# First expert layer: gate and up weights in blocks of 128 rows by 2048 and 1536 columns, and overflow products at the head of every other chunk

## The reference, cut to what matters

```python
def swiglu(h, w_in, w_out):
    gate, up = jnp.split(h @ w_in, 2, axis=-1)
    return (jax.nn.silu(gate) * up) @ w_out

for e in range(N_EXPERTS):          # 8 experts, D_FF = 3584
    y = y + gates[:, e:e + 1] * swiglu(hf, w_in[e], w_out[e])
```

## Time and profile before

| | |
|---|---|
| median of three runs | 1984.08 us (1981.81 to 1988.30) |
| span of the profiled execution | 1985.8 us; the page gives no other time of it |
| TensorE matmuls busy | 1831.9 us, 92% |
| VectorE, ScalarE, GpSimd busy | 610.9, 479.7 and 350.8 us |
| read from HBM | 579.96 MB, 293 GB/s over the span |
| mean granted TensorE clock | 0.954 of full speed |

### The profile page before, as it was taken

How to read it: one execution, slowest core, us unless ns; L and a number is a source line. 1 busy time by engine, 2 the same in 40 slices (tenths; PEclk the granted TensorE clock), 3 DMA queues, 4 the chain that set the end, 5 groups by cost and what they waited for, 6 DMA issues and landing times.

```text
span 1985.8 us, 28964 instructions
## 1 busy us (share of the span) xinstructions
PE 1831.9 (92%) x12157; PEld 1071.5 (54%) x12157; DVE 610.9 (31%) x1257; ACT 479.7 (24%) x813; POOL 350.8 (18%) x306
## 2 busy tenths in 40 slices
PE   8999999998996999999999999999995887699996
PEld 7987999776974433334333333233322887544442
DVE  6777545347465200100000000010002685600101
ACT  5854444315422110001000010000001564322120
POOL 3000000000000699999900000000001000000000
PEclk9998999998998899999999999999998897889999
DMA  6455665436525999999999999999995440579995
GB/s 187 154 147 179 207 204 204 159 119 243 193 89 211 391 410 405 419 413 410 404 416 416 410 410 397 419 410 411 404 420 189 140 152 11 212 288 419 419 420 234
DMA packets 185008, 583.04 MB, mean 294 GB/s; under 512 B 11162, under 2 KB 77355, under 8 KB 158241
## 3 DMA queue, kind: packets, MB, share of 16 engines
q1 hardware_dynamic: 182256, 575.09, 75.3%
q0 software_dynamic: 2608, 5.97, 1.1%
HBM read 579.96 MB, written 1.05 MB: 293 GB/s over the span
## 4 chain that ended last, share of the span: by engine, by line
PE 72%; DMA 12%; DVE 10%; ACT 3%; issue 2%; SPq 0%; DVEq 0%; ACTq 0%
PE ps L1708 18%; PE ps L435 8%; PE ps L436 8%; PE ps L437 8%; DMA ring<-in_moe_w_out 7%; PE ps L2147 6%; PE ps L1713 5%; PE ps L1744 4%; DMA ring<-in_moe_w_in 3%; PE ps L2171 3%; DVE wlo L468 2%; PE ps L1749 1%; DMA more<-in_moe_w_in 1%; PE ps L604 1%; PE ps L2114 1%
## 5 line engine op out<-in xcount | busy, mean ns | idle before, releaser
L1708 PE MATMUL ps<-ring,xg 128*64 128x512 f32 x1624 | 411.3, 602 | 13.0 <-ACT sgm L1818 5.8
L468 DVE TENSOR_TENSOR wlo<-raw,whi 128x2048 fp32r<-128x2048 f32 (+6 forms) x97 | 213.8, 2208 | 190.0 <-ACT whi L460 189.8
L1708 PEld LDWEIGHTS ps<-ring,xg 128*64 128x64 f32 x1624 | 122.2, 137 | 219.3 <-issue 207.8
L460 ACT ACTIVATE whi<-raw 128x2048 fp32r<-128x2048 f32 (+6 forms) x97 | 178.8, 1845 | 182.3 <-PE ps L437 80.6
L435 PE MATMUL ps<-xh,whi 128*128 128x272 f32 (+1 forms) x712 | 212.1, 298 | 4.4 <-DVE xl L535 4.3
L1744 PE MATMUL ps<-ring,ahm 128*64 128x512 f32 x824 | 204.5, 598 | 11.4 <-DMA ring<-in_moe_w_out 8.9
L437 PE MATMUL ps<-xh,wlo 128*128 128x272 f32 (+1 forms) x712 | 209.7, 295 | 0.0
L436 PE MATMUL ps<-xl,whi 128*128 128x272 f32 (+1 forms) x712 | 209.4, 294 | 0.0
L2080 POOL TENSOR_SCALAR lnt<-lnt,h 128x384 f32<-128x384 f32 x120 | 188.3, 1569 | 12.2
L1882 DVE TENSOR_TENSOR sgm<-sgm,ps 128x512 f32<-128x512 f32 x28 | 18.2, 685 | 512.0 <-PE ps L1713 512.0
L715 POOL DMA_DIRECT2D lnt<-in_ln_gain x4 | 2.2, 559 | 819.7 <-issue 524.9
(11 more groups left out here) (572 smaller groups left out, 2439.6 us busy)
## 6 DMA issues: line engine op xcount, KB each, us to landing
ring<-in_moe_w_in SPq DMA_DIRECT2D x203, 1024.0 KB, 17.9
ring<-in_moe_w_out SPq DMA_DIRECT2D x103, 1024.0 KB, 19.9
ring<-in_w_gate SPq DMA_DIRECT2D x29, 1024.0 KB, 13.4
raw<-in_ffn_w_in SPq DMA_DIRECT2D x28, 1024.0 KB
ring<-in_w_down SPq DMA_DIRECT2D x26, 1024.0 KB, 13.0
raw<-in_w_ada SPq DMA_DIRECT2D x24, 1024.0 KB
more<-in_moe_w_in SPq DMA_DIRECT2D x21, 1024.0 KB, 18.1
ring<-in_w_up SPq DMA_DIRECT2D x20, 1024.0 KB, 11.6
```

The lines of the kernel that those rows point to most:

```text
L460: e.activation(whi[0:rows, s % NSPL, 0:n], raw[0:rows, i % NRAW, 0:n], ACT.Copy).then_inc(S.hi.s, S.hi.up((s,)))
L468: e.tensor_tensor(wlo[0:rows, s % NSPL, 0:n], raw[0:rows, i % NRAW, 0:n], whi[0:rows, s % NSPL, 0:n].bitcast(F32), ALU.subtract).then_inc( ...
L1708: e.matmul(ps_[b][64 * v:64 * v + 64, :], a[:, kk_, 64 * v:64 * v + 64], both[v][:, k, 512 * b:512 * b + 512], start=kk_ == 0, stop=kk_ == 7)
```

## The change

There are two column groups now, 2048 and 1536 wide, and a chunk of gate or up is one block of 128 rows: 8 KB or 6 KB in one piece to a partition. A pass has 16 steps of the first and 16 of the second group, and 14 of down as before. Gate and up of the first group take five PSUM banks each. The overflow products of a chunk are four matmuls of 512 or 384 columns, in place of eight of 256 or sixteen of 128. In every other step (j odd), in down too, the overflow products come first and the main ones after them. The hidden tiles `sgm` and `sgo` are twice as large, and transposes are done once after the first group and once in down.

```diff
-GROUPS = [(0, 1024), (1024, 1024), (2048, 1024), (3072, 512)]
+GROUPS = [(0, 2048), (2048, 1536)]
...
-                o, m = o + (3584 if nm == "u" else 0), 2048 // n
-                part = lambda v: w_in[bass.ds(v, 1), 128 * m * j:128 * m * j + 128 * m, o:o + n].rearrange("e (k p) n -> p (e k) n", p=128)
+                o, m = o + (3584 if nm == "u" else 0), 1
+                part = lambda v: w_in[bass.ds(v, 1), 128 * j:128 * j + 128, o:o + n].rearrange("e (k p) n -> p (e k) n", p=128)
...
-            return a[:, 256 * c:256 * c + 256] if n == 1024 else a.rearrange("p (j q i) -> p j i q", j=2, i=2)[:, c // 2, c % 2, :]
+            return a[:, 512 * c:512 * c + 512] if n == 2048 else a.rearrange("p (s j q i) -> p j i s q", j=2, q=128, i=2)[:, c // 2, c % 2]
...
+                    ps_, po = [], None
+                    for j in range(8):
+                        both = pair_weights(e, C, SLOTS1, (key, x, nm, gi, j), 1)
+                        for what in ("mo", "om")[j % 2]:
+                            if what == "o":
+                                po = po or bk.take(e, key, nm + "o", x, gi)
+                                for c in range(4):
+                                    ins = e.matmul(po[32 * c:32 * c + 32, 0:n // 4], a[:, j, 128:160], quarter(both[0][:, 0, :], n, c),
+                                                   start=j == 0, stop=j == 7)
+                                continue
                             for b in range(n // 512):
+                                if j == 0:
+                                    ps_.append(bk.take(e, key, nm, x, gi, b))
                                 for v in range(2):
+                                    ins = e.matmul(ps_[b][64 * v:64 * v + 64, :], a[:, j, 64 * v:64 * v + 64],
+                                                   both[v][:, 0, 512 * b:512 * b + 512], start=j == 0, stop=j == 7)
...
                 both = pair_weights(e, C, SLOTS1, (key, x, "d", 0, j), 2)
+                for what in ("mo", "om")[j % 2]:
...
                 if j == 0:
-                    turn(x, 3)
+                    turn(x, 1)
```

More of the change, by code:

```diff
@@ L259, in chunk @@
                 o, n = GROUPS[gi]
-                o, m = o + (3584 if nm == "u" else 0), 2048 // n
-                part = lambda v: w_in[bass.ds(v, 1), 128 * m * j:128 * m * j + 128 * m, o:o + n].rearrange("e (k p) n -> p (e k) n", p=128)
-            pieces = lambda s, v: [(s.rearrange("p (k n) -> p k n", k=m), part(v))]
-            S.add((key, x, nm, gi, j, u), 128, CW, pieces, split=False)
+                o, m = o + (3584 if nm == "u" else 0), 1
+                part = lambda v: w_in[bass.ds(v, 1), 128 * j:128 * j + 128, o:o + n].rearrange("e (k p) n -> p (e k) n", p=128)
+            w = CW if nm == "d" else n
+            pieces = lambda s, v: [(s[:, 0:w].rearrange("p (k n) -> p k n", k=m), part(v))]
+            S.add((key, x, nm, gi, j, u), 128, w, pieces, split=False)
         for x in range(NP1):
-            steps = [(nm, gi, j) for gi, (_, n) in enumerate(GROUPS) for nm in "gu" for j in range(n // 256)]
+            steps = [(nm, gi, j) for gi in range(len(GROUPS)) for nm in "gu" for j in range(8)]
             steps += [("d", 0, j) for j in range(14)]
@@ L1665, in turn @@
             e.wait_ge(C.dve.s, C.dve.at(key, "mulo", x, gi))
-            v = w["sgo"][:, 0:n // 4].rearrange("p (q i) -> p i q", i=n // 512)
             for i in range(n // 512):
-                ins = e.transpose(p[:, 128 * i:128 * i + 128], v[:, i, :], idn)
+                a = w["sgo"][:, 256 * (i // 2):256 * (i // 2) + 256] if n == 2048 else w["sgo"][:, 128 * i:128 * i + 128]
+                ins = e.transpose(p[:, 128 * i:128 * i + 128], a.rearrange("p (q i) -> p i q", i=2)[:, i % 2, :] if n == 2048 else a, idn)
             ins.then_inc(C.pe.s, C.pe.up((key, "turno", x, gi)))
@@ L1734, in down @@
             for j in range(14):
[L1735 to L1738, removed]
+                if j % 8 == 0:
+                    for b in range(GROUPS[j // 8][1] // 512):
+                        e.wait_ge(C.act.s, C.act.at(key, "ah", x, j // 8, b))
+                    e.wait_ge(C.act.s, C.act.at(key, "aho", x, j // 8))
                 both = pair_weights(e, C, SLOTS1, (key, x, "d", 0, j), 2)
[L1740 to L1744, removed]
-                                     both[v][:, i, 512 * q:512 * q + 512], start=f == 0, stop=f == 27)
-                for q in range(2):
-                    for i in range(2):
-                        c = 2 * q + i
+                for what in ("mo", "om")[j % 2]:
+                    for i in range(2):
+                        f = 2 * j + i
+                        for q in range(2):
+                            for v in range(2 if what == "m" else 0):
+                                ins = e.matmul(D[q][64 * v:64 * v + 64, :], w["ahm"][:, f, 64 * v:64 * v + 64],
+                                               both[v][:, i, 512 * q:512 * q + 512], start=f == 0, stop=f == 27)
+                    for c in range(4 if what == "o" else 0):
+                        q, i = c // 2, c % 2
                         ins = e.matmul(Do[32 * c:32 * c + 32, :], w["aho"][:, 2 * j + i, :], both[0][:, i, 512 * q:512 * q + 512],
@@ L1793, in turn @@
             e.wait_ge(C.pe.s, C.pe.at(key, "turno", x, gi))
-            e.activation(w["aho"][:, f:f + 4 * m, :].rearrange("p (c i) n -> p i c n", i=m),
+            v = w["aho"][:, f:f + 4 * m, :]
+            e.activation(v.rearrange("p (c i) n -> p i c n", i=4) if n == 2048 else v.rearrange("p (i c) n -> p i c n", c=4),
                          bk(key, "turno", x, gi)[:, 0:128 * m].rearrange("p (i c n) -> p i c n", i=m, c=4),
@@ L1801, in up @@
                 for nm in "gu":
-                    for j in range(n // 256):
+                    for j in range(8):
                         step += 1
@@ L1815, in up @@
                             if gi or x:
-                                y_, g_ = (x, gi - 1) if gi else (x - 1, 3)
+                                y_, g_ = (x, gi - 1) if gi else (x - 1, 1)
                                 e.wait_ge(C.pe.s, C.pe.at(key, "turno", y_, g_))
```

18 lines of the change are left out of this document (2 added, 16 removed).

## The result

The changed kernel took 1966.93 us (median of 4 runs, 1966.16 to 1967.33) against 1986.19 us (1981.81 to 1989.71) for the kernel before beside it: 0.9911 of its time [0.9892, 0.9930]. Forecast were 1970.1 us with a range of 1964 to 1981. The time fell into the range and close to the forecast, but the trace shows that two of its parts are off, in opposite directions: the first expert layer gained 9.9 us and not 14, and what comes behind the layer, of which the prediction said nothing, gained as well. That the sum came out close is therefore luck in part.

The account below looks back on a forecast made before the run. The prediction took the DMA queue's time for all weight bytes as the bound: 16.0 us saved by longer rows less 2.0 us of empty queue gives 14.0, so 1984.1 - 14.0 = 1970.1 us, range 1964 to 1981.

Parts of the forecast that it names:

- The queue's speed: First expert layer's weight transfers: 420.5 GB/s at 8 KB rows, 417 at 6 KB, saving 4.0 us a pass, 16.0 in four.
- Rival 1: Gate and up transfers: row length doesn't count at this pitch, speed stays 411 GB/s, time about 1980 us; chance 14%.
- times per row: Queue's time per row and engine: 84.5 ns at 2048 B, 159.5 at 4096 B, 311.7 at 8192 B.
- TensorE hidden: First expert layer: TensorE needs 206.2 us a pass, under the queue's 209.9, so its savings and new waits are worth nothing.
- Rival 2: Where PSUM bank sets are reused: TensorE becomes the bound, 2013 us at full price, 1998 at three quarters; chance 6%.
- I take 2.0 us, once: Pass 0, around the second slot release: the queue stands empty for 0 to 4 us, taken as 2.0 us lost.
- 6 us for an order that saves nothing: Pass 0: the queue's empty time would be 6 us if TensorE saved none of its 0.15 us a step.
- Rival 3: Ring runs empty in every pass, some 2 us each: 1976 us, or 1984 with 4 us gaps; chance 7%.

Follow-up runs that it names:

- the half rows: Changed kernel with each gate and up chunk loaded by two DMAs of half the columns (4 KB and 3 KB rows); 1979.68 us, 0.9987 of before.
- the run with the gathering late: Changed kernel with selection and gathering for the next pass moved from steps 10 to 14 to steps 26 to 30; 1963.86 us, 0.9899 of before.
- the blocks alone: Changed kernel with the main products first in every step, so only the new blocks are left of the change; 1969.86 us, 0.9934 of before.
- the four shifted kernels: Changed kernel with 8, 16, 32 or 48 more VectorE instructions in pass 1, shifting later VectorE code; 1970.25, 1964.02, 1961.72 and 1972.04 us.
- order only: Kernel before with only the order changed: overflow products first in every other step, down too; 1982.98 us, 1.0005 of before.

## Why the prediction was right, and where it was not

**The queue's speed** was right. Forecast were 420.5 and 417 GB/s, measured 420 and 416; passes 1 to 3, taken from the times at which 88, 176, 264 and 350 MB had come, became shorter by 3.8 to 4.4 us each (forecast 4.0). Rival 1 falls with these speeds and with the half rows. (The prediction's own times per row give 7.3 and 9.5 ns a row beside its bytes, where it says 7 to 9; its forecast does not use that figure.) The rule of the Trainium skill (DMA: Bandwidth & Descriptors, Specifications) that rows from 512 B on move at line rate does not agree with the runs: 401 to 403, 410 and 420 at 3, 4 and 8 KB of the same weights. The 1 MiB a DMA of the Trainium skill (DMA: Bandwidth & Descriptors, Rules for kernel authors) was not needed here: 0.75 MiB chunks ran at 416 in a full queue.

**TensorE hidden** was right: steps of 4.44 us as forecast, two 1536-wide ones in 5.30 + 1.49 us (3.40 each, forecast 3.37), and a wait of 0.88 us for the first bank of the second group (forecast 0.9). Rival 2 didn't come; the chain meets transfers in passes 1 to 3.

**"I take 2.0 us, once"** is the term that was mis-sized. By the stretches from 730 to 760 us the queue moved 0.71, 0.50, 0.61, 0.36 and 0.25 MB less than at 420 GB/s, together 2.43 MB or 5.8 us. TensorE's side of that step was right: it freed the slots of the seventeenth step at 742.8 (forecast 741.7, and the layer began 1.1 us later), the next at 748.8, half of 5.30 behind 746.19 (forecast 747.9). The queue's side was not, in two ways. I let it begin between 642 and 648; in the stretch from 635 to 640 it already moved 229 GB/s before (the row below) and 149 after, so it began some 4 us earlier than the earliest that I allowed. By the stretches of after 8.3 MB had come by 660, 16.6 by 680 and 37.5 by 730; the 42.2 MB were due at 741, ahead of all of the 742 to 748. And I let the shortage end with the one late release, while half of the loss lies behind 745: the stretches are still at 348 and 371 GB/s between 750 and 760, while TensorE frees one pair of slots after another. Why the queue is slower with so little in hand is not shown; the run with the gathering late shows only that the loss goes when TensorE is earlier. The prediction's 6 us for an order that saves nothing was off as well: sixteen steps of 0.15 us are 2.4 us more and not 4, and the blocks alone lost 1.7 us more than after (7.7 and 6.0). The layer so gained 9.9 us; without the shortage, in the run with the gathering late, 14.8. The 14.0 forecast lie between. The row of before:

```profile
635.00:640.00 5.00, 0.00 (x0) 0.00 (x0) 4.66 (x15) 0.00 (x0) 0.00 (x0) 0.50 0.66 229
```

Rival 3 came only in small: of the later passes one, pass 2, shows a shortage, of under 1 us.

**What was not forecast** is the time behind the layer, 481.9 us before (1503.94 to 1985.8) and 470.4 after. Of these 11.5 us, 5.3 are the shorter way from the last addition to the norm's gain (15.4 and 10.1), that is, the second wait. Another 7.3 lie between the norm and the second expert layer's first product (211.1 and 203.8 us), and go with the clock; 1.2 are lost again between the last step and the last addition. The rows have the columns as above, and the stretches of after are set 13 us earlier, as far as its norm lies ahead. Before:

```profile
1628.00:1668.00 40.00, 31.08 (x176) 26.84 (x173) 29.86 (x64) 24.63 (x96) 0.00 (x0) 0.73 0.15 56
1668.00:1768.00 100.00, 78.70 (x390) 56.87 (x392) 40.12 (x131) 28.86 (x56) 5.04 (x8) 0.82 0.44 169
```

After:

```profile
1615.00:1655.00 40.00, 29.75 (x206) 25.63 (x205) 30.62 (x70) 25.78 (x96) 0.00 (x0) 0.88 0.19 68
1655.00:1755.00 100.00, 79.04 (x414) 53.55 (x413) 40.15 (x131) 29.61 (x58) 5.05 (x8) 0.86 0.51 200
```

In these two executions the records of the granted clock show TensorE for 88 us (before) and 65 us (after) at the lower level, 1.2 GHz, between the layer and the second expert layer. But this is no property of the change: after itself, run again, had 72, and the four shifted kernels 82, 65, 65 and 82. Over the fourteen traces the way from the norm's gain to the second expert layer tends to be longer the more of it runs at the lower level, from 203.8 us with 58 us of it (after) to 211.1 with 78 (before); one trace with 58 us of it has 206.7. Against all runs of before (medians of 1983.0 and 1983.3 over 23 and 15 of them) after's 1966.9 and 1968.4 are some 15 to 16 us better: about 10 from the layer by its trace, 5 from the second wait. The forecast of 14 so came true as a sum of 10 and 5. That is luck in part: the shortage took 3.8 us more than the prediction allowed, and a gain behind the layer, which it put at nothing without a reason, made up for it.

## What to carry to other kernels

Where a full queue sets the time, look at the rows of the blocks: longer rows are worth a few per cent of the transfer time even in the range of kilobytes, and splitting each in two takes it back. A ring that is counted in slots and not in bytes holds less when the blocks shrink; find where the consumer is furthest behind and move its side work away from there before counting the gain. And look at what follows the changed stretch: it can gain or lose time there that the change itself did not aim at.

## What was not expected of the hardware

- At the jump over code that is not run VectorE waits 4.25 to 4.48 us in every trace that has it; without it 0.26 us pass in the two traces that don't. A second wait of 5.52 (before) or 4.14 us (order only) lies between statistics instructions, and packets of the kind "instruction" land 1.6 us ahead of its end.
- 8 KB rows at a pitch of 28 KB are as fast as blocks in one piece: 420 and 420 to 421 GB/s.
- Executions of almost the same kernel differ by 10 us (1961.7 to 1972.0 in the four shifted ones), with layers within 1.5 us. Most of the rest is when the layer begins (655.2 to 659.8 us) and the way from the norm to the second expert layer (203.8 to 209.0 us), which goes with the time at the lower clock.
